# A hybrid denoising step in fp32: first-layer columns turned from SBUF, and a later release of the fourth expert's weights

## The reference, cut to what matters

```python
sh1, sc1, g1, sh2, sc2, g2 = split(silu(cond) @ w_mod[i] + b_mod[i], 6)   # one set for c, one for c_ctx
h = rmsnorm(x, norm_mix[i]) * (1 + sc1) + sh1
x = x + g1 * mixer(h)
h = rmsnorm(x, norm_ffn[i]) * (1 + sc2) + sh2
x = x + g2 * moe(h)            # 16 experts, 2 for each token, chosen by a router
```

## Time and profile before

| | us |
|---|---|
| median of 3 runs (lowest, highest) | 1713.58 (1707.59, 1720.03) |
| the profiled execution, its own time | 1713.52 |
| its span | 1711.7 |
| PE busy | 1460.2 (85%) |
| DVE, ACT, POOL busy | 542.7, 374.9, 196.9 |

### The profile page before, as it was taken

How to read it: one execution, slowest core, us unless ns; L and a number is a source line. 1 busy time by engine, 2 the same in 40 slices (tenths; PEclk the granted TensorE clock), 3 DMA queues, 4 the chain that set the end, 5 groups by cost and what they waited for, 6 DMA issues and landing times.

```text
span 1711.7 us, 26512 instructions
## 1 busy us (share of the span) xinstructions
PE 1460.2 (85%) x10765; PEld 878.6 (51%) x10765; DVE 542.7 (32%) x1326; ACT 374.9 (22%) x985; POOL 196.9 (12%) x287
## 2 busy tenths in 40 slices
PE   2889898698998898698889988969989899969983
PEld 1766685232576576332374455843327666763321
DVE  0125614111526524111333243232115146251104
ACT  0104512111211622111120333111112035221101
POOL 0100021010213011110110000210111000120002
PEclk9889999899998999899999999989999999989997
DMA  9797035899959224899948323468997850339993
GB/s 337 282 323 257 2 137 207 327 418 422 362 200 323 48 99 156 326 398 421 385 175 272 79 74 111 159 240 355 421 407 269 292 164 2 123 137 361 422 418 108
DMA packets 125059, 428.70 MB, mean 250 GB/s; under 512 B 13123, under 2 KB 55062, under 8 KB 100358
## 3 DMA queue, kind: packets, MB, share of 16 engines
q1 hardware_dynamic: 96854, 350.32, 53.6%
q0 software_dynamic: 21136, 72.73, 12.4%
q10 hardware_dynamic: 6944, 3.91, 0.8%
HBM read 389.22 MB, written 40.26 MB: 251 GB/s over the span
## 4 chain that ended last, share of the span: by engine, by line
PE 67%; DMA 13%; DVE 8%; issue 5%; POOL 2%; ACT 2%; ACTq 1%; SPq 0%; DVEq 0%; POOLq 0%
PE bank L1668 59%; DMA work<-in_moe_w_gate 4%; PE bank L1831 3%; DMA ring<-in_w_mod 2%; DMA h_slots<-xn,row_of 2%; DMA hT<-h_slots 2%; PE bank L1991 2%; POOL h_slots L799 1%; ACTq L591 1%; PE bank L1725 1%; ACT pp L1020 1%; POOL small L694 1%; DVE xn L1167 1%; PE bank L1876 1%; DVE gbc L1164 1%
## 5 line engine op out<-in xcount | busy, mean ns | idle before, releaser
L1668 PE MATMUL bank<-ring,pp 128*32 128x512 f32 x2312 | 324.0, 608 | 13.0 <-issue 10.9
L1668 PE MATMUL bank<-ring,hT 128*128 128x256 f32 (+3 forms) x1142 | 273.8, 400 | 5.9 <-DVE kT L1433 2.6
L1668 PEld LDWEIGHTS bank<-ring,hT 128*128 128x128 f32 x1142 | 214.7, 197 | 62.4 <-issue 29.4
L1668 PE MATMUL bank<-work,pp 128*32 128x512 f32 x888 | 238.5, 621 | 3.1 <-DVE pp L1542 2.4
L1668 PE MATMUL bank<-ring,xn 128*128 128x256 f32 x768 | 168.2, 380 | 0.0
L1668 PEld LDWEIGHTS bank<-ring,pp 128*32 128x32 f32 x2312 | 89.1, 112 | 138.3 <-issue 137.3
L1668 PEld LDWEIGHTS bank<-ring,xn 128*128 128x128 f32 x768 | 145.0, 190 | 19.4
L1668 PE MATMUL bank<-V,pp 128*32 128x512 f32 x640 | 119.4, 615 | 25.5 <-issue 21.5
L1558 DVE TENSOR_TENSOR pp<-bank,pp 128x256 f32<-128x256 f32 x40 | 17.0, 425 | 341.5 <-ACT pp L1097 341.5
L1668 PE MATMUL bank<-ring,condT 128*32 128x256 f32 x1536 | 97.6, 400 | 16.9 <-DMA ring<-in_w_mod 16.9
L1020 ACT ACTIVATE pp<-bank,neg_max 128x384 f32<-128x384 f32 x192 | 95.8, 515 | 13.8 <-DVE neg_max L1449 10.1
(11 more groups left out here) (249 smaller groups left out, 1553.3 us busy)
## 6 DMA issues: line engine op xcount, KB each, us to landing
ring<-in_w_mod SPq DMA_DIRECT2D x96, 1024.0 KB, 9.0
ring<-in_moe_w_down SPq DMA_DIRECT2D x52, 1024.0 KB, 16.9
ring<-in_moe_w_gate SPq DMA_DIRECT2D x32, 1024.0 KB, 11.7
ring<-in_moe_w_up SPq DMA_DIRECT2D x32, 1024.0 KB, 12.2
hT<-h_slots POOLq DMA_DIRECT2D x36, 512.0 KB, 11.7
V<-in_moe_w_gate SPq DMA_DIRECT2D x16, 1024.0 KB, 13.5
V<-in_moe_w_up SPq DMA_DIRECT2D x16, 1024.0 KB, 16.9
work<-in_moe_w_gate SPq DMA_DIRECT2D x16, 1024.0 KB, 9.7
```

The source lines that it names most:

```text
L1668: return pe.matmul(out, lhsT, rhs, start=start, stop=stop)
```

## The change

1. In layer 0, POOL's load of shift and scale back from DRAM is dropped. PE turns `m_out` itself, as four transposes of 128x128 (two vectors, two halves of the 256 columns), as soon as ACT has copied it. DVE picks the two used columns out of each group of 32 with two copies. The stores to `m_all` stay. The counts of `mod_cols_in` fall by one load everywhere, and the wait of `load_columns` on `mod_ready` is dropped for the second set of layer 0.
2. In every layer SP waits ahead of expert 3 for the rows of block 1 to have landed in SBUF (`g_in[1]`, which counts the loads of blocks 1, 3, 5, 7 and 9, so five of them a layer), where it waited for the scatters.

```diff
                 for key in moe_units(L):
                     if key == ("moe_g", L, 3):
-                        sp.wait_ge(h_out, 96 * (L + 1))
+                        sp.wait_ge(g_in[1], 16 * (BLOCKS // 2 * L + 1))
...
             def load_columns(L, s):
                 wait_mod_stored(pool, L, 3 * s + 1)
-                if L > 0:
+                if L + s > 1:
                     pool.wait_ge(mod_ready, 2 * L + s - 1)
...
             for L in range(DEPTH):
                 s, kind = STACK[L], KINDS[L]
-                if L == 0:
-                    load_columns(0, 0)
                 for b in range(NB):
                     norm_power(2 * L, b)
...
+                elif s == 0:
+                    key = ("modc", 0, 0)
+                    wait_bank_full(dve, key)
+                    for v in range(2):
+                        last = V_.tensor_copy(modc[:, v].rearrange("p (t h) c -> p h t c", h=2),
+                                              job_bank(key)[:, 2 * v * P:2 * (v + 1) * P].rearrange(
+                                                  "p (h t r) -> p h t r", h=2, t=4)[:, :, :, 0:2])
+                    free(last)
+                    dve.wait_ge(freed_v, jobs[key][2])
...
                 if L == 0:
-                    mod_columns(0, 0)
+                    key = ("modc", 0, 0)
+                    wait_bank_free(pe, key)
+                    for v in range(2):
+                        pe.wait_ge(mod_copied, v + 1)
+                        for h in range(2):
+                            at = (2 * v + h) * P
+                            ins = pe.transpose(job_bank(key)[:, at:at + P], m_out[:, v, h * P:(h + 1) * P], ident[:, :])
+                    done(ins)
```

More of the change, by code:

```diff
@@ L1714, in mod_columns @@
                 wait_bank_free(pe, key)
-                pe.wait_ge(mod_cols_in, 16 * (2 * L + s + 1))
+                pe.wait_ge(mod_cols_in, 16 * (2 * L + s))
                 done(pe.transpose(job_bank(key)[:, 0:32], m_in[:, s, :], ident[0:32, 0:32]))
@@ L2082, in turn_columns @@
                 def turn_columns():
-                    pe.wait_ge(mod_cols_in, 16 * (2 * (L + 1) + 1))
+                    pe.wait_ge(mod_cols_in, 16 * (2 * (L + 1)))
                     pe.wait_ge(lateT_ready, 2 * (L + 1))
```

## The result

The changed kernel takes 1690.91 us (median of 3 runs, 1690.53 to 1692.6), the kernel before 1713.58. The ratio is 0.9858, with a 95% interval of 0.9815 to 0.9902. (Ratios here are those that come with the runs and not exactly the quotient of the two medians, which is 0.9868; where a gain is given "by the ratio", it is the time before times one less the ratio.) The forecast was 1693.5 us. Measured again on another chip the ratio was 0.9866 (0.9836 to 0.9895). The profiled execution has a span of 1690.4 us, 21.3 less than before.

The account below looks back on a forecast made before the run. PE work holds 67% of the chain, DMA 13%; quick gains lie where PE waits on a DMA, and the weight stream paces each layer's end. Opening 8 plus rows 12 gives 20 us: 1693.5 us, 8-in-10 range 1685 to 1706.

Parts of the forecast that it names:

- The opening: Part 1, layer 0's start: columns turned on PE without store and load start the first projection earlier; 8.0 us gained.
- a clock that falls: Opening: PE's pauses around the turn lower its granted clock again; taken as the case, with 8.0 us gained.
- the worst case: Opening: the first projection starts inside the low-clock stretch and may lose up to 1 us more than before.
- my low end of 7.2: Opening: gain of about 7.2 us if the clock falls and the first projection loses up to 1 us more.
- a clock that stays high: Opening: at 2.4 GHz the turn gains a further 0.93 and the first projection 1.79 us, 10.9 in all.
- The DMA idle time that was to absorb the shift: From 70 to 84 us the DMA engines idle 11.6 us for lack of slots; slots freed 8 us earlier fill 8.
- The rows: Part 2, block 1 of each layer: with weights held back, the rows land in 4.4 us; part worth 12 us.
- My lower bound of 3.7: Block 1's rows: landing at best, 2.5 us fixed as for a lone 1 MB unit plus 1.2 for half a megabyte.
- The rival that rows are slow by themselves: Block 1: rows alone still take 6.4 to 7.6 us, part 2 worth 1 to 3 us, time 1703; chance 14%.
- equal shares: Slow-rows rival's premise: each queue gets an equal share, so weights cost two blocks of rows at most 2.4 us.
- The stretches: Block 1 to each layer's late weights: stream ends earlier by idle time less 1.8 us: 3.9, 4.2, 3.5, 0.2.
- The slower rival: SP's wait in each layer: held weights starve the stream if rows land from about 8 us on; 1724 us, chance 5%.

Follow-up runs that it names:

- the run with 12 products: Changed kernel plus 12 needless 128x128 products on PE behind the four transposes, to fill PE's pause in the opening: 1697.89 us, ratio 0.9842.
- the two runs with 12 products: Changed kernel plus 12 needless PE products, once alone (ratio 0.9842), once with SP waiting only for the issue of blocks 1 and 2's loads (0.9839).
- two units ahead: Changed kernel, but expert 3's gate and up wait only for the scatters, the rest for block 1's rows: 1720.46 us, ratio 0.9978.
- the hold alone: Kernel before with only SP's wait for block 1's rows, columns still by way of DRAM: 1701.65 us, ratio 0.9921.
- the hold in three layers: Changed kernel with SP's wait for block 1's rows in layers 0 to 2 only, layer 3 waiting for the scatters: 1699.43 us, ratio 0.9900.
- both runs with products: Changed kernel plus needless 128x128 products on PE in the opening: 24 of them (1686.55 us, ratio 0.9863) or 12 (1697.89 us, ratio 0.9842).
- the columns alone: Changed kernel with SP waiting for the scatters again, so only columns turned from SBUF remain: 1710.94 us, ratio 0.9962.
- the misplaced wait: Changed kernel with the rows' wait moved to expert 3's down, where it held nothing that mattered: 1706.46 us, ratio 0.9965.
- the run that releases at issue: Changed kernel, but SP waits only until POOL has issued the loads of blocks 1 and 2: 1693.2 us, ratio 0.9865.
- one unit ahead: Changed kernel, but expert 3's gate waits only for the scatters, its up and the rest for block 1's rows: 1708.56 us, ratio 0.9907.
- long hold: Changed kernel, but SP waits until PE has turned the rows of block 2: 1728.52 us, ratio 1.0099.

## Why the prediction was right

**The opening.** I had the turn at 38.28 us, the first projection at 41.9 and 8.0 us in all. Measured: 38.83, 41.56, and 9.0 us by the load of layer 0. Nine profiles with the new columns and without the extra products have it between 293.4 and 297.4 us, the two without them at 303.9 and 304.6. The choice of a clock that falls was right, and the run with 12 products shows both halves of it: the pause is the cause, and it costs 2.6 us on the spot. The fall also costs what I gave for the worst case: the first projection takes 1.0 us longer than before, so at the second block's projections 7.5 us are left of the gain (59.66 against 52.13), near my low end of 7.2. Which of 7.5 and 9.0 lasts these profiles can't tell, as the nine loads lie 6.5 to 10.5 us before 303.94. So 8.0 was right within that spread, and its closeness is partly luck. For a clock that stays high I had 10.9 us less a wait of about 1 us for the early `w_mod` units; the two runs with 12 products wait 0.51 and 1.03 us there, and their loads come 10.3 and 8.9 us before 303.94. The DMA idle time that was to absorb the shift did so: from 70 to 84 us the share is now

```profile
70.00:84.00 14.00, 14.00 (x110) 10.73 (x112) 1.41 (x3) 0.96 (x2) 0.00 (x0) 1.00 0.71 260
```

where it was 0.19.

**The rows.** I took 4.4 us; they land in 3.6 to 4.0. My lower bound of 3.7, from a lone megabyte, was the better value: block 2's load, issued 0.6 to 0.8 us behind, has taken a few tenths at most. The fit of the Trainium skill ("DMA: Bandwidth & Descriptors", section "Anatomy of one DMA — SWDGE (gpsimd) path"), an estimate of 3.2 us, is 0.4 to 0.8 too short here. The rival that rows are slow by themselves needed 6.4 to 7.6 us for rows alone, and is refuted by the 3.6 to 4.0. Its equal shares are refuted too: one megabyte ahead costs 2.5 us and two cost 5.0, which is their own time at 422 GB/s, so it is what stands ahead that counts. The Trainium skill's rule of queues in turn ("DMA: Bandwidth & Descriptors", section "Queues, rings and completion order") doesn't foresee this, and the measurement decides.

One reading of mine was too coarse. I had five units start at the very event that releases the rows. The timeline of the kernel before has only two of them close to POOL's load, and by the runs with one and two units ahead it is these two that cost the 5 us:

```profile
303.67 0.33 SPq L602 DMA_DIRECT2D ring<-in_moe_w_gate  x1
303.94 1.16 POOL L806 DMA_DIRECT2D hT<-h_slots  x2 [12.26 <-DMA h_slots<-xn,row_of]
304.04 0.43 SPq L602 DMA_DIRECT2D ring<-in_moe_w_up  x1
```

**The stretches.** I had 3.9, 4.2, 3.5 and 0.2 us; the profile after has 4.2, 3.8, 3.5 and -1.3. Over six profiles that hold until the landing (two of the changed kernel, the hold alone, the hold in three layers, and both runs with products) the mean stretch of layers 0 to 2 is 97.0 us. Over four that don't hold (the kernel before, the columns alone, the misplaced wait, two units ahead) it is 101.5. So 4.5 us a layer, 13.4 in all, beside 11.6 predicted.

The reason that I gave for the size was that a full stream sets the end of the stretch, that its idle time of 5.7, 6.0 and 5.3 us would close, and that the hold would cost it 1.8 us. The idle time can be read from the profiles in the way of my text, length times 1.02 less the share (the last column but one). The first 9 us from the load and the next 42 us of layer 0, in the kernel before, the changed kernel and the run that releases at issue:

```profile
303.94:312.94 9.00, 0.18 (x1) 0.19 (x2) 0.00 (x0) 0.00 (x0) 1.15 (x2) 0.50 0.93 359
312.94:354.94 42.00, 41.44 (x340) 15.01 (x343) 9.04 (x19) 6.36 (x14) 2.88 (x6) 0.92 0.89 347
```

```profile
294.90:303.90 9.00, 4.80 (x30) 2.80 (x34) 0.69 (x1) 0.86 (x2) 1.67 (x3) 0.56 0.80 292
303.90:345.90 42.00, 42.00 (x376) 14.38 (x369) 8.35 (x18) 5.88 (x13) 3.89 (x7) 1.00 1.01 411
```

```profile
293.55:302.55 9.00, 4.55 (x22) 2.65 (x26) 0.69 (x1) 0.86 (x2) 1.68 (x3) 0.52 0.86 341
302.55:344.55 42.00, 42.00 (x376) 14.11 (x369) 8.36 (x18) 5.49 (x12) 3.90 (x7) 1.00 1.01 405
```

The same, as means of layers 0 to 2, in us; behind these 51 us the DMA engines are full in all six, within 0.4 us:

| run | rows land after | idle, first 9 us | idle, next 42 us | stretch |
|---|---|---|---|---|
| before | 8.9 | 0.8 | 5.7 | 101.4 |
| two units ahead | 8.9 | 1.1 | 3.9 | 101.7 |
| one unit ahead | 6.3 | 1.8 | 1.1 | 98.9 |
| released at issue | 4.1 | 1.5 | 0.7 | 97.3 |
| changed kernel | 3.8 | 2.0 | 0.4 | 97.6 |
| long hold | 3.7 | 4.7 | 8.5 | 107.3 |

The stretch less the idle time is 94 to 97 us in all six. So the stretch is the time that the engines need for its transfers plus their idle time, as I had it. The hold costs 1.2 us of stream at its start (I had 1.8) and closes 5.3 us of idle time behind it (I had 5.7). The late gate shows the same: in layer 0 it is issued 76.8 us after the load, 6.4 us sooner than before, but lands only 4.2 us sooner, since it takes 20.62 us to land and not 18.39.

The table also has the answer to the runs in which the stream starts early. With the release at issue, 0.5 us less is idle at the start and 0.3 us more behind it: so the hold until the landing had little left to give back. With units ahead of the rows, the rows are late, and the idle time behind the restart comes back. In it SP waits for slots that PE has yet to free: the next unit behind the five, into `work`, is issued 20.9 us after the load of layer 0 in the kernel before, and 20.4, 17.4, 15.0 and 14.5 us in the next four rows of the table. That is 11 to 12 us behind the landing of the rows each time, wherever the stream started.

**The slower rival.** Its place was right and its condition isn't met: the rows land in 3.6 to 4.0 us. Held by 12.4 us more, the kernel is 38 us above the changed one and above the kernel before by 1%. Its price was some 2 us a layer too high: a stream that starts 16.0 - 2.4 = 13.6 us later should have made the stretch of layer 0 13.6 - 5.7 = 7.9 us longer than before, and it is 5.6 us longer.

**Open.** Where the remaining 2 us of the first profile come from isn't settled; the pieces between the stretches vary by several us in profiles that are equal there (293.9, 291.1 and 301.1 us ahead of layer 3). Whether layer 3 gains or loses is below what these profiles can tell.

## What to carry to other kernels

When an engine waits for a small load, look at what is issued within a microsecond around it: here it was enough to hold back the large transfers by less than a microsecond, until the small one was issued, and a wait for its landing was not needed. What is issued last before the release, here block 2's load, loses time all the same, so put the urgent load first. Then ask what idle time the held stream has behind it; here a hold of 3.6 us cost 1.2 us of stream and closed 5.3 us of idle time, and one of 16 us cost 10 us a layer. And a short pause of TensorE can cost twice, once in itself and once in the clock behind it (here 2.6 us); how much of the second part is still there 250 us later these runs can't tell.

## What the runs showed of the hardware

I had not expected order to be so sharp across two queues. A 512 KB load issued by POOL 0.27 us after a 1 MB unit of SP and 0.1 us before the next one lands behind both: 8.1 to 9.2 us. With the first of the two alone it is 6.0 to 6.4 us. With SP's units behind it, the first 0.86, 0.79, 0.46 and 0.46 us later in the four layers, it lands in 3.8, 4.1, 4.5 and 4.9 us, beside 3.6 to 4.0 with nothing behind it. So here a POOL load lost a whole unit's time, 2.5 us, to what SP issued 0.1 us later, some 0.5 to 0.9 us to what came 0.46 us later, and next to nothing to what came 0.86 us later. A load that stands second on POOL's queue is worse off: block 2's, issued within 0.4 us of two of these units, landed in 7.9 to 8.6 us, and in 4.1 to 4.7 where nothing of SP's was near it.
